# Projection Z and attention A of a hybrid diffusion block: two blocks of engine programs written as one

## The chip, the cores and the metric

The kernel runs on one core of one Trainium2 chip. The metric is the device time of one execution in microseconds (us). Three executions of the kernel before took 1727.18, 1730.48 and 1730.88 us, median 1730.48. A fourth one was profiled: it took 1729.09 us, of which its trace spans 1727.3 us.

The engines are named as in the profile: PE is TensorE (matmuls and transposes), PEld its weight loads, DVE is VectorE, ACT is ScalarE, POOL is GpSimd, SP is the sync engine, which here issues DMAs. Each engine runs its own list of instructions in order and waits on semaphores for the others. A wait at the head of an engine's list holds up everything that stands behind it in that list.

## The reference

One layer of a transformer: 128 context tokens and 512 latent tokens (640 in all, five tiles of 128), D_MODEL 1024. What matters here:

```python
z = h @ lw['w_in']
q_a, k_a, v_a, c_q, c_kv, k_r, g_a, g_b = jnp.split(z, cuts, axis=-1)
qa = rmsnorm(q_a.reshape(b, s, H_A, HD_A), lw['gqa_qn']).transpose(0, 2, 1, 3)
ka = rmsnorm(k_a.reshape(b, s, KV_A, HD_A), lw['gqa_kn']).transpose(0, 2, 1, 3)
...
qa = apply_rope(qa, *rope_a)              # latent tokens only
...
o_a = block_attention(...)                # attention A: 8 heads, 2 key heads, 128 wide
...
qb = (cq @ lw['w_qb'])...                 # queries of attention B
o_b = block_attention(...)                # attention B
merged = sigmoid(g_a) * (o_a @ w_oa) + sigmoid(g_b) * (o_b @ w_ob)
x = x + g1 * (merged @ w_out)
x = x + g2 * moe_ffn(...)                 # 64 small experts and a shared one
```

Context tokens attend to context keys only (128 columns of scores), latent tokens to 128 cached keys and 512 latent ones (640 columns).

## The kernel before

The kernel is a row of blocks. In each block every engine has one program, and all engines meet at the block's end. The blocks around the change are Z (lines 422 to 720), attention A and attention B (one function, `attend`, line 749; A is called first), and a block between A and B that expands B's keys.

**Z** computes the first 1984 columns of `w_in` in four chunks (`CHUNKS`: queries of heads 0 to 3, keys and values, the latent columns, queries of heads 4 to 7) and for five token tiles each: 20 units, `UNITS[i] = (chunk, tile)`, in this order. Unit i goes through these steps:
- `project(i)` on PE (line 451): 24 matmuls of 512 columns into PSUM bank i % 4.
- `squares(i)` on ACT (line 515), `sums(i)` on DVE (line 626), a power on POOL (line 594): the reciprocal norms.
- `apply(i)` on DVE (line 641): norm, gain and rotation, five vector operations for queries. It ends with semaphore `s_zn`.
- `turn(i)` on PE (line 472): four transposes into bank 4 + i % 2, semaphore `s_zT`.
- `untangle(i)` on ACT (line 538): one copy out of PSUM into `qT`, semaphore `s_ze`.

They are staggered: on PE `turn(i - 2)` follows `project(i)`, on DVE `apply(i - 1)` follows `sums(i)`, on ACT `untangle(i - 3)` follows `squares(i)`. So after `project(19)` each engine still has a tail: `turn(17)`, `turn(18)`, `turn(19)` on PE, `apply(18)` and `apply(19)` on DVE, `untangle(16)` to `untangle(19)` on ACT. Units 18 and 19 are tiles 3 and 4 of the last chunk: queries of heads 4 to 7. The split of heads 0 and 1 into high and low parts is made in Z by POOL (lines 602 to 604).

**A** works on 40 tiles n = (head, token tile), `N = 40`, with `lag = 2`. For each n:
- PE, loop at line 896: `scores(n)`, `turn_p(n - 2)` (transposes of the probabilities), `values(n - 3)` (probabilities times values), and at the last tile of a head, for heads 0 to 4, `rope_rows(h)` (line 819): four f32 matmuls of 512 columns with the weights `wqb`, for attention B.
- ACT, loop at line 949: `take_p(n - 2)`, `softmax(n)` (the exponential with a row sum), and the copies of a finished output.
- DVE, loop at line 1127: `maximum(n)`, `take_p(n - 2)`, `normalise(n)` (a reciprocal and a scaling).
- `maximum(n)` waits for `scores(n)`, `softmax(n)` for `maximum(n)`, `normalise(n)` for `softmax(n)`.
- PSUM: scores lie in banks 0 and 1 or 2 and 3 in turn (the 128 columns of tile 0 in bank 0 or 2), transposed probabilities in banks 4 and 5, outputs in bank 6 (`pO`) and bank 7 (`pC`, `rope_rows`).

`wqb` (1.5 MB) is loaded by SP at the start of A's block, line 795. Its place in SBUF is that of Z's scratch rows (`zq`, `zn`, `zt`, `rot`), so it can't be loaded before Z's rows are done with. `rope_rows(0)` waits for the load (`s_wqb`, line 822).

Of the kernel before, what the change touches and what calls it, by code (L numbers as in the profile page):

```python
# [26 lines left out]
F32 = mybir.dt.float32  # L27
# [7 lines left out]
P = 128  # L35
# [59 lines left out]
def build(nc, I, O, S, ctx):  # L95
# [326 lines left out]
    with nc.Block() as block:  # L422
        @block.sync
        def _(sp):
            sp.dma_start(wz[1], w_in_v[:, :, C_KA:C_KA + 512]).then_inc(s_wz[1], 16)
            for g in range(KVA):
                sp.dma_start(cache[:, g * HD:(g + 1) * HD], I["cache_gqa_k"][0, 0, g]).then_inc(s_cache, 16)
                sp.dma_start(vA[:, 1, g, :], I["cache_gqa_v"][0, 0, g]).then_inc(s_vc, 16)
            sp.dma_start(cache[:, 256:384], I["cache_mla_ckv"][0, 0]).then_inc(s_cache, 16)
            for c in (384, 448):  # L430
                sp.dma_start(cache[:, c:c + ROPE], I["cache_mla_krope"][0, 0]).then_inc(s_cache, 16)
            sp.dma_start(kgB, I["mla_kva_g"].to_broadcast([P, KVL])).then_inc(s_cache, 16)
            sp.dma_start(wkvb, I["w_kvb"][0]).then_inc(s_wkvb, 16)

            sp.wait_ge(s_z, NT)
            sp.dma_start(wz[0][:, :, 0:448], w_in_v[:, :, C_CQ:C_CQ + 448]).then_inc(s_wz[2], 16)
            sp.wait_ge(s_z, 2 * NT)
            sp.dma_start(wz[1], w_in_v[:, :, 512:1024]).then_inc(s_wz[3], 16)

            sp.wait_ge(s_zn, NT + 1)  # L440
            for g in range(KVA):
                sp.dma_start(O["gk"][0, 0, g], zo[0][:, g * HD:(g + 1) * HD]).then_inc(s_out, 16)
                sp.dma_start(O["gv"][0, 0, g], vA[:, 0, g, :]).then_inc(s_out, 16)
            sp.wait_ge(s_zn, 2 * NT + 1)
            sp.dma_start(O["ckv"][0, 0], zo[1][:, 256:256 + KVL]).then_inc(s_out, 16)
            sp.dma_start(O["kr"][0, 0], zo[1][:, 384:384 + ROPE]).then_inc(s_out, 16)
            sp.wait_ge(s_out, 16 * 6)

        @block.tensor
        def _(pe):  # L450
            def project(i):

                c, t = UNITS[i]
                w, b = CHUNKS[c][2], c % 2
                if i >= 4:

                    pe.wait_ge(s_zn, i - 3)
                if c == 0:
                    pe.wait_ge(s_hl, t + 1)
                elif t == 0:  # L460
                    pe.wait_ge(s_wlP, 4 + KT * c)
                out = bank(i % 4)[:, 0:w]
                for k in range(KT):
                    if i == 0:
                        pe.wait_ge(s_wlP if k % 2 else s_wlV, k // 2 + 1)
                    xh, xl = hHi[:, k, t * P:(t + 1) * P], hLo[:, k, t * P:(t + 1) * P]
                    pe.matmul(out, xh, zHi[b][:, k, 0:w], start=(k == 0), stop=False)
                    pe.matmul(out, xl, zHi[b][:, k, 0:w], start=False, stop=False)
                    mm = pe.matmul(out, xh, zLo[b][:, k, 0:w], start=False, stop=(k == KT - 1))
                mm.then_inc(s_z, 1)  # L470

            def turn(i):

                pe.wait_ge(s_zn, i + 1)
                if i >= 2:
                    pe.wait_ge(s_ze, i - 1)
                    if remainder_of(i - 2):
                        pe.wait_ge(s_zl, remainder_of(i - 2))
                kind = CHUNKS[UNITS[i][0]][0]
                src = out_rows(i)  # L480
                for j in range({"q": 4, "kv": 2, "lat": 4}[kind]):
                    tr = pe.transpose(bank(4 + i % 2)[:, j * P:(j + 1) * P], src[:, j * P:(j + 1) * P], ident[:, :])
                tr.then_inc(s_zT, 1)

            def turn_cache():

                pe.wait_ge(s_cache, 16 * 6)
                for j in range(4):
                    tr = pe.transpose(bank(6)[:, j * P:(j + 1) * P], cache[:, j * P:(j + 1) * P], ident[:, :])
                tr.then_inc(s_zc, 1)  # L490

            n = len(UNITS)
            for i in range(n):
                project(i)
                if i == 1:
                    turn_cache()
                if i >= 2:
                    turn(i - 2)
            turn(n - 2)
            turn(n - 1)  # L500

        @block.scalar
        def _(act):
            def rows_hi(t):

                act.activation(hHi[:, :, t * P:(t + 1) * P], hT[:, :, t * P:(t + 1) * P], ACT.Copy).then_inc(s_hh, 1)

            def weights_hi(c, k0, k1):

                w, b = CHUNKS[c][2], c % 2  # L510
                act.wait_ge(s_wz[c], 16)
                for k in range(k0, k1):
                    act.activation(zHi[b][:, k, 0:w], wz[b][:, k, 0:w], ACT.Copy).then_inc(s_wh, 1)

            def squares(i):

                c, t = UNITS[i]
                kind = CHUNKS[c][0]
                n = {"q": 512, "kv": 256, "lat": 448}[kind]
                act.wait_ge(s_z, i + 1)  # L520
                if i >= 2:

                    act.wait_ge(s_zm, i - 1)
                if kind == "kv":
                    act.activation(vA[:, key_col(t) // P, :, :].rearrange("p g d -> p (g d)"),
                                   bank(i % 4)[:, 256:512], ACT.Copy)
                act.activation(zq[i % 2][:, 0:n], bank(i % 4)[:, 0:n], ACT.Square).then_inc(s_zq, 1)

            def take_latent(ps, col):

                act.activation(ckvT[:, col:col + P], ps[:, 2 * P:3 * P], ACT.Copy)
                return act.activation(krHH[:, col:col + P], ps[:, 3 * P:4 * P], ACT.Copy)

            def take_keys(ps, col):

                return act.activation(kHiA[:, :, col:col + P], ps[:, 0:256].rearrange("p (g t) -> p g t", g=KVA), ACT.Copy)

            def untangle(i):

                c, t = UNITS[i]  # L540
                kind = CHUNKS[c][0]
                act.wait_ge(s_zT, i + 1)
                ps = bank(4 + i % 2)
                if kind == "q":
                    h = 4 * (c // 3)
                    ins = act.activation(qT[:, h:h + 4, t * P:(t + 1) * P], ps.rearrange("p (h t) -> p h t", h=4),
                                         ACT.Copy)
                elif kind == "kv":
                    ins = take_keys(ps, key_col(t))
                else:  # L550
                    for j in range(2):
                        act.activation(cqT[:, j, t * P:(t + 1) * P], ps[:, j * P:(j + 1) * P], ACT.Copy,
                                       scale=cols[:, 80 + j:81 + j])
                    ins = take_latent(ps, key_col(t))
                ins.then_inc(s_ze, 1)

            rows_hi(0)
            weights_hi(0, 0, KT)
            rows_hi(1)
            n = len(UNITS)  # L560
            for i in range(n):
                c, t = UNITS[i]
                if i + 2 < NT:
                    rows_hi(i + 2)
                squares(i)
                if i == 1:
                    act.wait_ge(s_zc, 1)
                    take_keys(bank(6), P)
                    take_latent(bank(6), P).then_inc(s_cc0, 1)
                if i >= 3:  # L570
                    untangle(i - 3)
                if t in AHEAD and c < 3:

                    if c == 0 and t == 3:
                        act.wait_ge(s_gd, 1)
                    weights_hi(c + 1, *AHEAD[t])
            for i in range(n - 3, n):
                untangle(i)

        @block.gpsimd  # L580
        def _(pool):
            def weights_lo(c, ks):

                w, b = CHUNKS[c][2], c % 2
                for k in ks:
                    pool.wait_ge(s_wh, KT * c + k + 1)
                    pool.tensor_tensor(zLo[b][:, k, 0:w], wz[b][:, k, 0:w], zHi[b][:, k, 0:w].bitcast(F32),
                                       ALU.subtract).then_inc(s_wlP, 1)

            weights_lo(0, range(1, KT, 2))  # L590
            for i, (c, t) in enumerate(UNITS):
# [3 lines left out]
                if t in AHEAD and c < 3:  # L595
                    weights_lo(c + 1, range(*AHEAD[t]))
# [1807 lines left out]
```

## Time and profile before

| | us |
|---|---|
| executions | 1727.18, 1730.48, 1730.88 (median 1730.48) |
| the profiled execution | 1729.09 |
| its span | 1727.3 |
| PE busy | 1551.4 (90%) |
| DVE busy | 1016.0 (59%) |
| ACT busy | 724.5 (42%) |
| POOL busy | 652.3 (38%) |
| last matmul of Z's projection starts | 178.19 |
| first matmul of A | 187.70 |

The profile names each instruction by its line in the kernel. Times start at the span's start. Busy time is the time in which an engine executed; the idle time in front of an instruction is given in square brackets with the instruction that ended it. PEclk is the share of TensorE's full clock that was granted: 1.0 is 2.4 GHz, 0.5 is 1.2 GHz.

### The profile page before, as it was taken

The page shows a single profiled execution, that of the slowest core. Times are in us where ns is not written, and L with a number is a line of the kernel's source. Part 1 is how long each engine was busy: PE and PEld are TensorE (multiplying, and loading weights), DVE is VectorE, ACT ScalarE, POOL GpSimd, SP SyncE. Part 2 cuts the span into 40 slices and gives each one's busy share as a digit, 9 for nine tenths or more (in the row PEclk, how much of TensorE's full clock was granted, in tenths as well). Part 3 has the DMA queues.
Part 4 walks back from the last instruction along what each step waited for, and adds up shares of the span by engine and source line. Part 5 has one row for each costly group of instructions (what it writes and reads, how often), then busy time and mean ns, then how long its engine had stood idle before and what let it go on. Part 6 is the DMA issues. An engine that isn't in the chain of part 4 may idle for free. (4 is left out here: it accounts for less than half of the span.)

```text
span 1727.3 us, 22786 instructions
## 1 busy us (share of the span) xinstructions
PE 1551.4 (90%) x7699; PEld 1169.3 (68%) x7699; DVE 1016.0 (59%) x1595; ACT 724.5 (42%) x1067; POOL 652.3 (38%) x727
## 2 busy tenths in 40 slices
PE   7799788799989999999896999999999999999992
PEld 2678687688879989964443766666666666666671
DVE  1966687666675565526643665555555555555554
ACT  2422343333442122202213565555555555555560
POOL 0445275322213233300452454344443434444561
PEclk9899899999999999999998999999999999999996
DMA  9320100000035464544174999999999999999954
GB/s 323 100 91 10 37 1 1 1 1 2 1 99 147 140 213 135 146 163 147 59 283 180 335 363 365 353 343 338 352 347 351 343 338 340 339 330 335 344 188 185
DMA packets 130282, 352.66 MB, mean 204 GB/s; under 512 B 22165, under 2 KB 77849, under 8 KB 103193
## 3 DMA queue, kind: packets, MB, share of 16 engines
q1 hardware_dynamic: 98488, 237.87, 37.8%
q10 hardware_dynamic: 10288, 71.86, 11.2%
q0 software_dynamic: 21440, 42.08, 9.7%
q8 instruction: 38, 0.62, 0.2%
q14 instruction: 28, 0.22, 0.0%
HBM read 335.53 MB, written 48.32 MB: 222 GB/s over the span
## 5 line engine op out<-in xcount | busy, mean ns | idle before, releaser
L2289 DVE TENSOR_TENSOR e_wlo<-mem,e_whi 128x2048 fp32r<-128x2048 f32 x140 | 314.6, 2289 | 98.6 <-ACT e_whi L2224 98.6
L2224 ACT ACTIVATE e_whi<-mem 128x2048 fp32r<-128x2048 f32 x140 | 260.2, 1913 | 24.4 <-DMA mem<-in_w_e 16.9
L2194 PE MATMUL psum<-mem 128*128 128x512 f32 x560 | 252.1, 593 | 2.1 <-ACT mem L2256 2.1
L2174 PE MATMUL psum<-e_whi,e_xhi 128*128 128x512 f32 x560 | 228.2, 408 | 7.1 <-DVE e_xlo L2296 7.1
L2176 PE MATMUL psum<-e_wlo,e_xhi 128*128 128x512 f32 x560 | 222.2, 397 | 0.0
L2175 PE MATMUL psum<-e_whi,e_xlo 128*128 128x512 f32 x560 | 222.0, 396 | 0.0
L2132 POOL TENSOR_TENSOR held<-nhalf 1x1 f32<-1x1 f32 x206 | 116.7, 567 | 261.3 <-DMA sums<-mem,si 104.4
L2194 PEld LDWEIGHTS psum<-mem 128*128 128x128 f32 x560 | 101.1, 190 | 103.0 <-issue 102.9
L1494 POOL TENSOR_TENSOR w_lo<-mem,w_hi 128x1024 fp32r<-128x1024 f32 x30 | 76.1, 2560 | 163.6 <-ACT w_hi L1438 163.6
L2296 DVE TENSOR_TENSOR e_xlo<-psum,e_xhi 128x512 fp32r<-128x512 f32 x140 | 90.2, 686 | 76.7 <-ACT e_xhi L2230 76.7
L2306 DVE TENSOR_TENSOR mem<-mem,psum 128x256 f32<-128x256 f32 x70 | 42.5, 607 | 151.0 <-ACT mem L2263 151.0
L2174 PEld LDWEIGHTS psum<-e_whi,e_xhi 128*128 128x128 f32 x560 | 105.8, 189 | 30.0 <-DVE e_xlo L2296 7.8
L2176 PEld LDWEIGHTS psum<-e_wlo,e_xhi 128*128 128x128 f32 x560 | 105.6, 189 | 25.5
L2175 PEld LDWEIGHTS psum<-e_whi,e_xlo 128*128 128x128 f32 x560 | 106.0, 189 | 22.3
L939 ACT ACTIVATE mem<-psum,small 128x640 f32<-128x640 f32 (+1 forms) x80 | 60.3, 754 | 130.4 <-DVE small L1106 87.9
L2182 PE MATMUL psum<-ident,mem 128*128 128x128 f32 x560 | 76.3, 280 | 43.1 <-DMA mem<-h,gi 34.4
L2230 ACT ACTIVATE e_xhi<-psum 128x512 fp32r<-128x512 f32 x140 | 76.0, 595 | 78.4 <-PE psum L2182 78.4
L2182 PEld LDWEIGHTS psum<-ident,mem 128*128 128x128 f32 x560 | 62.1, 142 | 68.0 <-DMA mem<-h,gi 56.0
L1513 DVE SCALAR_TENSOR_TENSOR mem<-mem,cols 128x256 f32<-128x256 f32 x256 | 107.7, 497 | 0.0
L1438 ACT ACTIVATE w_hi<-mem 128x1024 fp32r<-128x1024 f32 x30 | 30.2, 1054 | 165.2 <-DMA mem<-in_w_ob 90.8
L2147 POOL DMA_INDIRECT mem<-h,gi x68 | 75.9, 1116 | 36.4 <-issue 36.4
L1420 PE MATMUL psum<-h_hi,w_hi 128*128 128x320 f32 x256 | 81.7, 319 | 2.0 <-PEq L1149 2.0
(320 smaller groups left out, 3272.8 us busy)
## 6 DMA issues: line engine op xcount, KB each, us to landing
mem<-in_w_e SPq DMA_DIRECT2D x144, 1024.0 KB, 12.3
mem<-in_w_e ACTq DMA_DIRECT2D x66, 1024.0 KB, 11.2
mem<-in_w_mod SPq DMA_DIRECT2D x24, 1024.0 KB, 12.0
mem<-in_w_in SPq DMA_DIRECT2D x16, 512.0 KB, 4.5
mem<-in_w_in SPq DMA_DIRECT2D x3, 2048.0 KB, 8.8
sums<-mem SPq DMA_DIRECT2D x10, 512.0 KB, 4.7
mem<-sums SPq DMA_DIRECT2D x10, 512.0 KB, 5.4
mem<-in_x_sample SPq DMA_DIRECT2D x8, 512.0 KB, 11.0
```

The lines of the kernel that those rows point to most:

```text
L1420: pe.matmul(out, whi[b][:, q, k, :], hi[:, k, cols_], start=(k == 0), stop=False)
L1494: pool.tensor_tensor(wlo[b][:, q, :, :], wraw[b][:, q], whi[b][:, q, :, :].bitcast(F32), ALU.subtract).then_inc(sg["wl"], 1)
L1513: ins = dve.scalar_tensor_tensor(out=macc[b][y], in0=wmh[b][:, k, :], scalar=cols[:, k + 8 * y:k + 8 * y + 1], in1=brow[b] if k == 0 else ...
L2132: pool.tensor_tensor(held[:, c:c + 1], nhalf[0:1, 0:1], nhalf[0:1, 0:1], ALU.add)
L2174: pe.matmul(out, xh, wh, start=first, stop=False)
L2175: pe.matmul(out, xl, wh, start=False, stop=False)
L2176: return pe.matmul(out, xh, wl, start=False, stop=last)
L2182: tr = pe.transpose(pX[:, k * P:(k + 1) * P], xg[u % 2][:, k * P:(k + 1) * P], ident[:, :])
L2194: mm = pe.matmul(pY[:, cs], gT[:, f, :], w2[v][:, f, cs], start=(f == 0), stop=(f == 1))
L2224: act.activation(wHi13[u % 2][:, a], w13[u][:, a], ACT.Copy).then_inc(se["h13"], 1)
L2289: dve.tensor_tensor(wLo13[u][:, a], w13[u][:, a], wHi13[u % 2][:, a].bitcast(F32), ALU.subtract)\
L2296: dve.tensor_tensor(xLo[:, 4 * h:4 * h + 4, :].rearrange("p k t -> p (k t)"), pX[:, 512 * h:512 * (h + 1)], xHi[:, 4 * h:4 * h + 4, :].bit ...
```

## The change

Z's programs are no longer a block. They become functions (`zed_sync`, `zed_tensor`, `zed_scalar`, `zed_gpsimd`, `zed_vector`) that A's block calls at the head of each engine's program. Their text is the same, indented one level less, save for what follows.
- Units 18 and 19 are projected into banks 7 and 6 and transposed back into the same banks (`zbank`, `tbank`).
- The tail is cut. PE's Z program ends after `turn(17)`, DVE's after `sums(19)`, ACT's after `untangle(17)`.
- In A's loops `apply(18)` and `apply(19)` stand at the end of DVE's steps n = 1 and n = 2. `turn(18)` and `turn(19)` stand on PE in steps 3 and 4, between `turn_p(n - 2)` and `values(n - 3)`. `untangle(18)` and `untangle(19)` stand on ACT in steps 3 and 4 behind `softmax(n)`.
- New waits: `scores` of heads 0 and 1 wait for POOL's split (`s_qs`); `values(0)`, which writes bank 7, waits for `untangle(18)` and `values(1)`, which writes bank 6, for `untangle(19)`; POOL's split of head 4 waits for `untangle(19)`; SP's load of `wqb` waits for `turn(19)` (`s_zT` at 20).

The diff without the changes of indentation:

```diff
-    with nc.Block() as block:
-        @block.sync
-        def _(sp):
+    def zbank(i):
+        return bank(i % 4 if i < 18 else 25 - i)
+
+    def tbank(i):
+        return bank(4 + i % 2) if i < 18 else zbank(i)
+
+    def zed_sync(sp):
...
-                out = bank(i % 4)[:, 0:w]
+            out = zbank(i)[:, 0:w]
...
-            turn(n - 2)
-            turn(n - 1)
+        return turn
...
-            for i in range(n - 3, n):
-                untangle(i)
+        untangle(n - 3)
+        return untangle
...
-                    pool.wait_ge(s_qs, h + 1)
-                    pool.tensor_tensor(qLoA[:, h, :], qT[:, h, :], qHiA[h][:, :].bitcast(F32), ALU.subtract)
+                pool.wait_ge(s_qs, 2 * h + 1)
+                pool.tensor_tensor(qLoA[:, h, :], qT[:, h, :], qHiA[h][:, :].bitcast(F32), ALU.subtract)\
+                    .then_inc(s_qs, 1)
...
-                if i >= 1:
+            if 1 <= i < n - 1:
                     apply(i - 1)
...
-            apply(n - 1)
+        return apply
...
+        LASTZ = len(UNITS)
...
                 def _(sp):
+                    zed_sync(sp)
+                    sp.wait_ge(s_zT, LASTZ)
                     sp.dma_start(wqb, I["w_qb"][0].rearrange("(k p) n -> p k n", p=P)).then_inc(s_wqb, 16)
...
             def _(pe):
+                turn_z = None if mla else zed_tensor(pe)
...
                     elif t == 0 and h >= 2:
                         pe.wait_ge(s["ql"], h - 1)
+                    elif t == 0:
+                        pe.wait_ge(s_qs, 2 * h + 2)
...
+                        if not mla and h == 0:
+                            pe.wait_ge(s_ze, LASTZ - 1)
                         pe.matmul(pC, v[:, 0, :], pTc, start=True, stop=True).then_inc(s["C"], 1)
                         return
                     pe.wait_ge(s["TeA"], late(n))
+                    if t == 1 and not mla and h == 0:
+                        pe.wait_ge(s_ze, LASTZ)
...
                     if lag <= n < N + lag:
                         turn_p(n - lag)
+                    if not mla and n in (3, 4):
+                        turn_z(LASTZ + n - 5)
                     if n > lag:
                         values(n - lag - 1)
...
+                    if not mla and n in (3, 4):
+                        untangle_z(LASTZ + n - 5)
                     if n > lag:
                         h, t = TILES[n - lag - 1]
...
                         qh, ql, _ = q_of(h)
+                        if h == 4:
+                            pool.wait_ge(s_ze, LASTZ)
...
+                        if not mla and n in (1, 2):
+                            apply_z(LASTZ + n - 3)
                         if not mla and t == 2 and 1 <= h <= NT:
                             row_sums(h - 1)
```

## Rows read from the trace of the kernel before

**Rows 1.** Stretches of Z and of A: length, busy us (count) by engine, PEclk, DMA share, GB/s

```profile
170.00:178.00 8.00, 8.00 (x39) 6.54 (x38) 5.81 (x10) 1.09 (x2) 2.58 (x2) 1.00 0.00 0
187.60:335.00 147.40, 128.63 (x894) 116.48 (x894) 109.88 (x200) 62.26 (x152) 75.88 (x62) 0.99 0.03 12
```

**Rows 2.** Timeline of the seam: start us, us, engine, line, operation [idle before <-releaser]

```profile
178.43 0.60 PE L482 MATMUL psum<-ident,mem 128*128 128x128 f32 x4
179.12 1.08 ACT L546 ACTIVATE mem<-psum 128x512 f32<-128x512 f32 x2
...
179.98 0.17 DVE L639 TENSOR_SCALAR small<-small 128x4 f32<-128x4 f32 x1
...
182.79 0.68 DVE L666 TENSOR_TENSOR mem<-psum,small 128x512 f32<-128x512 f32 x1
...
184.90 0.69 DVE L672 TENSOR_TENSOR mem<-mem 128x512 f32<-128x512 f32 x1
...
185.65 1.12 PE L482 MATMUL psum<-ident,mem 128*128 128x128 f32 x4 [1.61 <-DVE mem L672]
186.80 0.60 ACT L546 ACTIVATE mem<-psum 128x512 f32<-128x512 f32 x1 [2.13 <-PE psum L482]
187.65 0.39 SPq L795 DMA_DIRECT2D mem<-in_w_qb  x1
187.66 1.28 ACT L939 ACT_TABLE_LOAD   x1 [0.27 <-PEq L422]
...
188.61 0.29 DVE L1102 TENSOR_REDUCE small<-psum 128x1 f32<-128x128 f32 x1 [3.02 <-PE psum L854]
...
190.32 0.82 DVE L1102 TENSOR_REDUCE small<-psum 128x1 f32<-128x640 f32 x1 [0.38 <-PE psum L854]
```

**Rows 3.** A's steps 1 to 3 on ACT and DVE, same view

```profile
191.18 0.79 ACT L939 ACTIVATE mem<-psum,small 128x640 f32<-128x640 f32 x1 [1.76 <-DVE small L1102]
...
192.10 0.16 DVE L1113 RECIPROCAL small<-small 128x1 f32<-128x1 f32 x1 [0.95 <-ACT mem L939]
...
192.29 0.55 DVE L1115 TENSOR_SCALAR mem<-mem,small 128x640 f32<-128x640 f32 x1
...
195.20 0.82 DVE L1102 TENSOR_REDUCE small<-psum 128x1 f32<-128x640 f32 x1
```

**Rows 4.** Scores of 640 columns, first and last of six matmuls: steps 1 and 3

```profile
188.38 0.57 PE L852 MATMUL psum<-ka_hi,qa_hi 128*128 128x320 f32 x1
...
189.81 0.47 PE L854 MATMUL psum<-ka_lo,qa_hi 128*128 128x320 f32 x1
...
194.64 0.39 PE L852 MATMUL psum<-ka_hi,qa_hi 128*128 128x320 f32 x1
...
195.46 0.31 PE L854 MATMUL psum<-ka_lo,qa_hi 128*128 128x320 f32 x1
```

**Rows 5.** TensorE's clock around the seam, columns as in rows 1

```profile
180.50:182.50 2.00, 0.00 (x0) 0.00 (x0) 1.93 (x5) 0.00 (x0) 0.73 (x1) 0.64 0.00 0
...
190.00:191.30 1.30, 1.30 (x7) 1.30 (x6) 0.82 (x1) 0.12 (x1) 0.00 (x0) 0.50 0.91 383
191.30:192.00 0.70, 0.49 (x4) 0.22 (x2) 0.00 (x0) 0.70 (x2) 0.00 (x0) 0.99 1.02 430
```

**Rows 6.** A's step 4 and the start of step 5, columns as in rows 2

```profile
196.72 0.74 PE L869 MATMUL psum<-ident,mem 128*128 128x128 f32 x5 [0.95 <-issue]
...
197.63 0.82 DVE L1102 TENSOR_REDUCE small<-psum 128x1 f32<-128x640 f32 x1
...
198.41 1.88 PE L825 MATMUL psum<-mem 128*128 128x512 f32 x4
...
200.61 0.29 DVE L1102 TENSOR_REDUCE small<-psum 128x1 f32<-128x128 f32 x1 [0.45 <-PE psum L854]
```

**Rows 7.** The load of wqb, issued at 187.65

```profile
DMA to landing us min/median/max: 6.4/6.4/6.4
```

**Rows 8.** SP's next issue behind it, in attention B

```profile
477.18 0.39 SPq L791 DMA_DIRECT2D mem<-in_w_in  x1
```

More of the change, by code:

```diff
@@ new lines, in zed_tensor, with project, turn, turn_cache @@
+    def zed_tensor(pe):
+        def project(i):
+            c, t = UNITS[i]
+            w, b = CHUNKS[c][2], c % 2
+            if i >= 4:
+                pe.wait_ge(s_zn, i - 3)
+            if c == 0:
+                pe.wait_ge(s_hl, t + 1)
+            elif t == 0:
+                pe.wait_ge(s_wlP, 4 + KT * c)
+            out = zbank(i)[:, 0:w]
+            for k in range(KT):
+                if i == 0:
+                    pe.wait_ge(s_wlP if k % 2 else s_wlV, k // 2 + 1)
+                xh, xl = hHi[:, k, t * P:(t + 1) * P], hLo[:, k, t * P:(t + 1) * P]
+                pe.matmul(out, xh, zHi[b][:, k, 0:w], start=(k == 0), stop=False)
+                pe.matmul(out, xl, zHi[b][:, k, 0:w], start=False, stop=False)
+                mm = pe.matmul(out, xh, zLo[b][:, k, 0:w], start=False, stop=(k == KT - 1))
+            mm.then_inc(s_z, 1)
+        def turn(i):
+            pe.wait_ge(s_zn, i + 1)
+            if i >= 2:
+                pe.wait_ge(s_ze, i - 1)
+                if remainder_of(i - 2):
+                    pe.wait_ge(s_zl, remainder_of(i - 2))
+            kind = CHUNKS[UNITS[i][0]][0]
+            src = out_rows(i)
+            for j in range({"q": 4, "kv": 2, "lat": 4}[kind]):
+                tr = pe.transpose(tbank(i)[:, j * P:(j + 1) * P], src[:, j * P:(j + 1) * P], ident[:, :])
+            tr.then_inc(s_zT, 1)
+        def turn_cache():
+            pe.wait_ge(s_cache, 16 * 6)
+            for j in range(4):
+                tr = pe.transpose(bank(6)[:, j * P:(j + 1) * P], cache[:, j * P:(j + 1) * P], ident[:, :])
+            tr.then_inc(s_zc, 1)
+        n = len(UNITS)
+        for i in range(n):
+            project(i)
+            if i == 1:
+                turn_cache()
+            if i >= 2:
+                turn(i - 2)
+        return turn
@@ new lines, in zed_scalar, with rows_hi, weights_hi, squares @@
+    def zed_scalar(act):
+        def rows_hi(t):
+            act.activation(hHi[:, :, t * P:(t + 1) * P], hT[:, :, t * P:(t + 1) * P], ACT.Copy).then_inc(s_hh, 1)
+        def weights_hi(c, k0, k1):
+            w, b = CHUNKS[c][2], c % 2
+            act.wait_ge(s_wz[c], 16)
+            for k in range(k0, k1):
+                act.activation(zHi[b][:, k, 0:w], wz[b][:, k, 0:w], ACT.Copy).then_inc(s_wh, 1)
+        def squares(i):
+            c, t = UNITS[i]
+            kind = CHUNKS[c][0]
+            n = {"q": 512, "kv": 256, "lat": 448}[kind]
+            act.wait_ge(s_z, i + 1)
+            if i >= 2:
+                act.wait_ge(s_zm, i - 1)
+            if kind == "kv":
+                act.activation(vA[:, key_col(t) // P, :, :].rearrange("p g d -> p (g d)"),
+                               zbank(i)[:, 256:512], ACT.Copy)
+            act.activation(zq[i % 2][:, 0:n], zbank(i)[:, 0:n], ACT.Square).then_inc(s_zq, 1)
+        def take_latent(ps, col):
+            act.activation(ckvT[:, col:col + P], ps[:, 2 * P:3 * P], ACT.Copy)
+            return act.activation(krHH[:, col:col + P], ps[:, 3 * P:4 * P], ACT.Copy)
+        def take_keys(ps, col):
+            return act.activation(kHiA[:, :, col:col + P], ps[:, 0:256].rearrange("p (g t) -> p g t", g=KVA), ACT.Copy)
+        def untangle(i):
+            c, t = UNITS[i]
+            kind = CHUNKS[c][0]
+            act.wait_ge(s_zT, i + 1)
+            ps = tbank(i)
+            if kind == "q":
+                h = 4 * (c // 3)
+                ins = act.activation(qT[:, h:h + 4, t * P:(t + 1) * P], ps.rearrange("p (h t) -> p h t", h=4),
+                                     ACT.Copy)
+            elif kind == "kv":
+                ins = take_keys(ps, key_col(t))
+            else:
+                for j in range(2):
+                    act.activation(cqT[:, j, t * P:(t + 1) * P], ps[:, j * P:(j + 1) * P], ACT.Copy,
+                                   scale=cols[:, 80 + j:81 + j])
+                ins = take_latent(ps, key_col(t))
+            ins.then_inc(s_ze, 1)
+        rows_hi(0)
+        weights_hi(0, 0, KT)
+        rows_hi(1)
+        n = len(UNITS)
+        for i in range(n):
+            c, t = UNITS[i]
+            if i + 2 < NT:
+                rows_hi(i + 2)
+            squares(i)
+            if i == 1:
+                act.wait_ge(s_zc, 1)
+                take_keys(bank(6), P)
+                take_latent(bank(6), P).then_inc(s_cc0, 1)
+            if i >= 3:
+                untangle(i - 3)
+            if t in AHEAD and c < 3:
+                if c == 0 and t == 3:
+                    act.wait_ge(s_gd, 1)
+                weights_hi(c + 1, *AHEAD[t])
+        untangle(n - 3)
+        return untangle
@@ L1061, in _ @@
             def _(dve):
+                apply_z = None if mla else zed_vector(dve)
                 def mean(h):
```

374 lines of the change are left out of this document (136 added, 238 removed).

## Prediction

> **What bounds the kernel now.** I read the stretches first, then the timeline of the seam between Z and A, then the clock, last the load of wqb. Z's projection keeps PE busy without a gap at the full clock: 8.00 of 8.00 us [rows 1]. A does not hang on PE's arithmetic but on a loop between DVE and ACT: maximum, exponential, reciprocal, scaling, next maximum. From maximum(2), which follows the scaling of 192.29 to 192.84, to maximum(3) at 195.20 it takes some 2.4 us a tile [rows 3]. So an instruction added to DVE's list in A costs its whole length, and PE costs something only where it comes late.
>
> Between the two lies the seam. `project(19)` and `turn(17)` end at 179.03. DVE goes on with `apply(18)` and `apply(19)` until 185.59, `turn(19)` ends at 186.77, ACT's `untangle(19)` at 187.40, A's block starts at 187.65, and DVE has its first maximum at 188.61 after 3.02 us of idleness. Then it waits 0.38 us more for PE, whose clock has fallen [rows 2, 5]. The 8.46 us from 180.15 (end of `sums(19)`) to 188.61 are thus 5.44 us of `apply` and 3.02 us of wait. The change can win the 3.02 and 0.38 at most; the `apply` work is moved, not removed.
>
> What is late by x us at the start of A makes the whole kernel late by x. SP's next issue stands at 477.18, behind A, in attention B [rows 8], and each block meets all engines at its end. I see nothing that would take it up.
>
> **The change, step by step.** I follow the new order with durations from the rows and put the result beside the times of before.
>
> DVE and ACT, steps 0 to 3. DVE is free at 180.15. `scores(0)` stands on PE right behind `turn(17)` (179.03) and needs under 1 us, so maximum(0) runs at 180.15 to 180.44. ACT is free at 180.20 and loads the exponential's table, 1.28 us [rows 2], until 181.50; before, this load lay beside PE's first scores. exp(0) (0.37 + 0.19 in the trace, some 0.5 overlapped, my estimate) ends at 182.0, reciprocal and scaling at 182.5. maximum(1) 0.82, exp(1) 0.92 with its row sum (191.18 to 192.10), reciprocal and scaling 0.74 [rows 3] end at 185.0. `apply(18)` takes 2.80 (182.79 to 185.59 for its twin [rows 2]), to 187.8. maximum(2), exp(2), normalise(2) take 2.55, to 190.4; `take_p(0)` lies in the wait for exp(2). `apply(19)` 2.80, to 193.2. maximum(3) runs at 193.2 to 194.0, where it was at 195.20 [rows 3]. Up to here the change **gains 2.0 us**.
>
> PE, step 3. PE waits in `turn_p(1)` for DVE's `take_p(0)` at 189.0, turns, does `turn(18)`, and stands in `values(0)`, which now waits for `untangle(18)`. This stands on ACT behind exp(3), which needs maximum(3): exp(3) ends at 194.95, the copy takes 0.60, PE goes on at 195.6. Queued behind `values(0)` are `scores(4)`. DVE would want them at 195.75 (exp(3), reciprocal, scaling). What they take depends on the clock. In the trace it fell in the idle stretch 180.5 to 182.5 (0.64 on the mean, PE idle since 179.03), and work from 187.70 on brought it back at 191.3 [rows 2, 5]. Here PE is idle from some 185.4 to 189.0 and from 191 to 195.6. I take 1.2 GHz. Six scores matmuls then take 1.90 (188.38 to 190.28), at 2.4 GHz 1.13 (194.64 to 195.77) [rows 4]; `values(0)` some 0.4. S(4) comes at 198.0 (197.1 at the full clock). maximum(4) starts at 198.0 against 197.63 before [rows 6]: the gain is gone, **+0.4**.
>
> PE, step 4. `turn_p(2)`: five transposes, 0.74 at the full clock [rows 6], some 1.35 at the half (four took 1.12 against 0.60 [rows 2]), to 199.35. `turn(19)` 0.6 to 1.1, its semaphore at 200.1. Only now may SP issue wqb: before, it did so at 187.65, and the 6.4 us to landing [rows 7] were over at 194.05, 4.4 us before `rope_rows(0)` at 198.41 [rows 6]. This cover is gone. Now it lands at 200.1 + 0.1 + 6.4 = 206.6. In the meantime `untangle(19)` behind exp(4) ends at 201.15 and `values(1)` at some 202.3. Then PE stands at `rope_rows(0)` for 4.3 us with all of head 1's scores queued behind it, and DVE and ACT wait for them.
>
> `rope_rows(0)` starts at 206.65 instead of 198.41: +8.2. After 4.3 us of idleness I take the half clock for its four matmuls of 512 columns. At the full clock they and the small `scores(5)` took 2.20 us (198.41 to maximum(5) at 200.61 [rows 6]), of which I give some 1.7 to the four; at the half clock these take twice as long: +1.7. maximum(5) comes at 210.6 instead of 200.61: **+10.0**. From there on every engine's order and distance is as before, with the clock back.
>
> Costed at nothing, with their cover: `scores(0)` and `scores(1)` wait for POOL's split, which POOL makes during units 16 and 17 of Z; POOL's split of head 4 waits for `untangle(19)`, at some 201, and isn't due for two heads; SP's other waits ahead of wqb are for units 5 and 10 of Z and their stores, long done; units 18 and 19 in other banks cost the same; one meeting of all engines less is in the 3.02. Bounds for what the trace doesn't show: the clock at `scores(4)` and at `rope_rows(0)` (the sum is +6.5 with 2.4 GHz at both, +8.2 at `rope_rows` alone with it, +10.0 with neither), and the load, alone on the queue as before, within 1 us of 6.4 to either side. A table load behind a busy ACT could also cost some wait in ACT's pipeline; at least 0, at most the 1.28 of the load again, since nothing longer of its kind is in the rows.
>
> The Trainium skill speaks against this order, in "DMA: Bandwidth & Descriptors", section "Rules for kernel authors": issue the DMA early, compute, and wait on its semaphore late, so that the fixed cost overlaps. The trace of before does this with 4.4 us to spare; the change issues the load immediately ahead of the one instruction that needs it.
>
> Of the exponential's table, the page "ScalarE: Activation LUTs", section "What ACT_TABLE_LOAD costs" of the Trainium skill, says about 2.66 us per switch, a drain of 1.38 included. The row has 1.28 and the exponential directly behind it; with the page's figure exp(0) and all that follows would come 1.4 later, and the sum would be +11.4. I keep the row's.
>
> The sum against the profiled execution: 1729.09 + 10.0 = 1739.1. This execution lies 1.4 below the median of the three; the mean of all four is 1729.4, which gives 1739.4. I say 1739.5.
>
> **The rivals.**
> (a) The load is exposed, but PE keeps the full clock at one or both places. For it: PE has short pieces of work in steps 1 to 3. Against it: the clock fell in the trace within 4 us of idleness [rows 5]. +6.5 to +8.2: 1736 to 1737.6.
> (b) The load is not what PE waits for, because it lands sooner or is issued sooner than I read. Then `rope_rows(0)` follows `values(1)` at 202.3 instead of 198.41: +3.9, 1733.3. Against it: 6.4 us measured, and the text of the wait.
> (c) Not slower: the turns moved into A are fully covered. The mechanism would be that DVE, not PE, is the last to be ready in steps 3 to 5, and only the gain of 2.0 stays: 1727.4. For it: DVE is A's bound over the stretch as a whole. It decides at `rope_rows(0)`: only if wqb lands before `values(1)` ends and `scores(4)` and `scores(5)` are done before DVE asks (195.75 and 198.3) is there no loss. Against it: both waits of PE are for copies that stand behind DVE's own chain, so PE can't be early.
> (d) A later stage takes up the delay (a stage bound by weight loads that begin at a fixed time): about 0, 1729.4. Against it: SP issues nothing between 187.65 and 477.18 [rows 8].
>
> **How the numbers follow.** The load exposed, half clock: 0.65. (a) 0.18. (b) 0.06. (c) 0.07. (d) 0.04. About 0.2%, 3.5 us, is what can be told from no change. The forecast and (a) are slower, 0.83, of (b) 0.04 is: 0.87. (c) at -2.0 is mostly within the bound, as are (d) and the rest of (b): same 0.09; faster 0.04, for (c) with the whole 3.4 us won. The range: executions of one kernel spread by 3.7 us, terms of the load and of the table by 1 to 1.4 each. From 1734, which takes in (a) and half of (b), to 1743.5: about 0.85.
>
> **What would show it.** In the profile after: wqb is issued right behind the last of the L482 transposes, about 12 us later than before and some 13 us after DVE's first maximum; PE has one idle piece of over 3 us that a DMA ends, in front of the first L825 matmul; PEclk is 0.5 around it; DVE's first maximum at about 180.2, its fourth at 193.2 or so, its sixth at about 210.6. Between A's sixth maximum and the end of A nothing changes its length. I'd be wrong if the first L825 matmul stood within 5 us of its old time, if PE's idle piece in front of it ended with an ACT copy, or if A's end moved by less than its sixth maximum.

## The result and the profile after

The changed kernel took 1738.75 us (median of 4 executions, 1735.91 to 1740.83) against 1729.87 for the kernel before (4 executions, 1727.18 to 1730.88). The ratio is 1.0053 with a 95% interval of 1.0034 to 1.0072: slower by half a per cent, some 9 us. The forecast was 1739.5, with 10.0 us for the seam. The profiled execution of the changed kernel took 1735.91, the shortest of its four, with a span of 1734.1.

The timeline of the seam in the changed kernel (start us, us, engine, line, operation [idle before <-releaser]; line 1126 is the maximum that stood at 1102, 666 the first product of `apply`, 547 `untangle`, 485 `turn`, 894 `values(0)`, 903 `values(1)`, 831 `rope_rows`), to be read against [rows 2, 3, 6]:

```profile
178.13 0.17 DVE L639 TENSOR_SCALAR small<-small 128x4 f32<-128x4 f32 x1
178.21 0.28 DVE L1126 TENSOR_REDUCE small<-psum 128x1 f32<-128x128 f32 x1
178.38 1.28 ACT L955 ACT_TABLE_LOAD   x1
...
180.16 0.16 DVE L1137 RECIPROCAL small<-small 128x1 f32<-128x1 f32 x1 [1.67 <-ACT mem L955]
...
183.00 0.68 DVE L666 TENSOR_TENSOR mem<-psum,small 128x512 f32<-128x512 f32 x1
...
188.16 0.68 DVE L666 TENSOR_TENSOR mem<-psum,small 128x512 f32<-128x512 f32 x1
...
190.88 0.82 DVE L1126 TENSOR_REDUCE small<-psum 128x1 f32<-128x640 f32 x1
...
192.52 0.59 ACT L547 ACTIVATE mem<-psum 128x512 f32<-128x512 f32 x1
...
193.25 0.77 PE L894 MATMUL psum<-mem 128*128 128x128 f32 x2 [4.21 <-ACT mem L547]
...
195.66 0.82 DVE L1126 TENSOR_REDUCE small<-psum 128x1 f32<-128x640 f32 x1 [2.25 <-PE psum L862]
196.48 1.06 PE L485 MATMUL psum<-ident,mem 128*128 128x128 f32 x4
...
197.62 0.39 SPq L799 DMA_DIRECT2D mem<-in_w_qb  x1
198.41 2.47 PE L903 MATMUL psum<-mem 128*128 128x128 f32 x10 [0.87 <-ACT mem L547]
205.15 3.78 PE L831 MATMUL psum<-mem 128*128 128x512 f32 x4 [4.27 <-DMA mem<-in_w_qb]
...
209.36 0.29 DVE L1126 TENSOR_REDUCE small<-psum 128x1 f32<-128x128 f32 x1 [10.80 <-PE psum L862]
```

The reader is to see four things. DVE no longer idles 3.02 us between Z and A: its first maximum follows the last sums at once. PE stands 4.21 us for `untangle(18)` and then makes the fifth maximum 2.25 us late. SP issues wqb only when `turn(19)` has ended, and PE waits 4.27 us for its landing. DVE, which had waited 0.45 us there, waits 10.80.

Two lines say how long the load took from issue to landing and where SP's next issue stands, against 6.4 [rows 7] and 477.18 [rows 8]:

```profile
DMA to landing us min/median/max: 7.5/7.5/7.5
```

```profile
484.78 0.39 SPq L793 DMA_DIRECT2D mem<-in_w_in  x1
```

TensorE's clock in the changed kernel (length, busy us and count by engine, PEclk, DMA share, GB/s), against [rows 5]:

```profile
178.00:180.20 2.20, 0.41 (x4) 0.15 (x2) 0.49 (x4) 2.10 (x4) 1.01 (x1) 1.00 0.00 0
180.20:182.40 2.20, 1.29 (x8) 1.01 (x8) 1.21 (x4) 0.88 (x2) 0.00 (x0) 0.85 0.00 0
182.40:185.00 2.60, 1.92 (x6) 1.51 (x6) 2.53 (x6) 0.00 (x0) 0.00 (x0) 0.50 0.00 0
...
200.90:205.10 4.20, 0.00 (x0) 0.00 (x0) 0.00 (x0) 0.00 (x0) 0.00 (x0) 0.50 0.57 235
205.10:209.00 3.90, 3.85 (x6) 1.79 (x7) 0.00 (x0) 0.00 (x0) 0.00 (x0) 0.50 0.00 0
```

It fell from 2.4 to 1.2 GHz at about 181.7 (which gives the mean of 0.85 in the second row). PE had been idle for 1.79 us, had worked from 180.18 to 181.43, and stood in a second gap, of 0.91 us. From 182.4 to 209.0 the mean PEclk is 0.50, so `values(1)`, the wait for the load and `rope_rows(0)` all lie at 1.2 GHz.

**One measure for all kernels.** The change touches little in front of the last sums of Z (two units use other banks) and nothing behind A's sixth maximum. So I measure the seam, from the start of the last L639 of Z to the start of A's sixth maximum. Before it is 200.61 - 179.98 = 20.63 us; after, 209.36 - 178.13 = 31.23: **+10.60**. From the sixth maximum to A's fortieth and last there are 95.66 us before and 95.67 after, so the later tiles take nothing up. The two spans differ by less (+6.8). Z's last sums came 1.85 us earlier in the profiled execution of the changed kernel (178.13 against 179.98), so the sixth maximum is 8.75 later. These 1.85 us arise where the clock differed in Z's first units: mean PEclk was 0.73 from 50 to 60 us and 0.85 from 90 to 100, against 0.59 and 0.71 before. No run ties them to the merge: the last sums stand at 179.98 and 179.43 in the two kernels with the old border, and between 177.96 and 180.04 in the eight merged ones. SP's issue in attention B is 7.60 later, so another 1.15 went behind A's sixth maximum. The stage behind A ran at a mean PEclk of 0.93 in the one execution (296 to 345 us) and 0.99 in the other (305 to 353), which fits, but no run tests it.

### The profile page after: what moved, and what is told of

Read it like the earlier page. It is cut to its first block and busy times, and to the rows that moved or that the text cites. A ratio compares the mean times of both kernels' runs of the same rounds, so it can differ in the third digit from the quotient of the medians.

```text
span 1734.1 us, 22778 instructions
## 1 busy us (share of the span) xinstructions
PE 1550.7 (89%) x7699; PEld 1169.1 (67%) x7699; DVE 1016.7 (59%) x1595; ACT 730.6 (42%) x1067; POOL 666.8 (38%) x727
## 5 line engine op out<-in xcount | busy, mean ns | idle before, releaser
L2158 POOL TENSOR_TENSOR held<-nhalf 1x1 f32<-1x1 f32 x206 | 126.7, 615 | 259.9 <-DMA sums<-mem_h,si 106.0
L903 PE MATMUL psum<-mem 128*128 128x128 f32 x640 | 83.9, 280 | 0.9 <-ACT mem L547 0.9
```

Source lines behind the costliest of these rows:

```text
L903: mm = pe.matmul(pO[:, (t - 1) * P:t * P], v[:, kt, :], pT[:, j, (t - 1) * P:t * P], start=(j == 0), stop=(j == 4))
L2158: pool.tensor_tensor(held[:, c:c + 1], nhalf[0:1, 0:1], nhalf[0:1, 0:1], ALU.add)
```

## The experiments

All seams below are from profiles of single executions. The work from the sixth maximum to the last, which no experiment touches, takes 95.6 to 95.8 us in every one of them. The seam itself varies more, because the clock does. The changed kernel and experiments 1, 3, 4 and 5 give PE the same work up to A's third scores, but the clock fell 3.6, 4.6, 3.7, 3.8 and 4.8 us behind Z's last sums. In experiment 1 it was back before `values(1)`, in the changed kernel and experiment 3 not, after the same work of PE. Where that matters, the text below says how much. Whole times tell less: executions of the kernel before spread from 1724.3 to 1732.2 beside the first four experiments and from 1724.0 to 1738.3 beside the others. L639 and the maximum carry other line numbers in each kernel; the sixth maximum of each is shown at the end.

**1. The rotary part of wqb early.** On the changed kernel:

```diff
+    wqr = mem.at(M_R + 9728, 2, HB, ROPE)
...
+        sp.wait_ge(s_z, 3 * NT)
+        for k in range(2):
+            sp.dma_start(wqr[:, k], I["w_qb"][0, k * P:(k + 1) * P].rearrange("p (h c) -> p h c", h=HB)[:, :, NOPE:NOPE + ROPE])\
+              .then_inc(s_wqr, 16)
...
-                        pe.wait_ge(s_wqb, 16)
+                        pe.wait_ge(s_wqr, 32)
...
-                                       wqb_rope[:, k], start=(k == 0), stop=(k == 1))
+                                       wqr[:, k], start=(k == 0), stop=(k == 1))
...
+                    pool.wait_ge(s_wqb, 16)
```

> The changed kernel with one thing taken off its path: the 64-column parts of the rotary queries in wqb (0.5 MB), which are all that rope_rows reads, are loaded into a place of their own as soon as unit 14 is projected; the whole wqb is loaded as in the changed kernel and waited for by POOL's late split alone. Measure: the seam, from the start of the last L639 of Z (sums(19)) to the start of A's sixth maximum: 20.63 us in the kernel before, 31.23 in the changed one. My theory (the load of wqb behind turn(19) is what PE waits for, 4.3 us of idleness plus a fallen clock): rope_rows(0) follows values(1) at once, the seam is 24.9, the time about 6 us below the changed kernel and some 3 to 4 above the kernel before. Rival (the waits for untangle(18) and untangle(19) are the cost, the load only lies beside them): the seam stays over 29 and the time within 2 us of the changed kernel.

Measured: seam 23.57 us, 7.66 below the changed kernel and 2.94 above the kernel before. Time: 1.0034 of the kernel before (1.0021 to 1.0048), some 5.9 us, where I had expected 3 to 4. PE in this kernel:

```profile
193.29 0.77 PE L899 MATMUL psum<-mem 128*128 128x128 f32 x2 [4.21 <-ACT mem L552]
...
196.46 0.60 PE L490 MATMUL psum<-ident,mem 128*128 128x128 f32 x4
198.34 1.35 PE L908 MATMUL psum<-mem 128*128 128x128 f32 x10 [1.28 <-ACT mem L552]
199.53 1.88 PE L836 MATMUL psum<-mem 128*128 128x512 f32 x4
```

`rope_rows(0)` (L836) now follows `values(1)` (L908) without a wait, at 1.88 us instead of 3.78. The two waits for copies (4.21 and 1.28) are still there. The rival that made the load a bystander falls.

The 7.66 us are three parts: 4.27 of PE's wait for the load, 2.00 from the start of `rope_rows(0)` to the sixth maximum at the faster clock, and 1.39 up to the end of `values(1)`. The third isn't the load's: the clock was back before `values(1)` (0.60 for `turn(19)`, 1.35 for `values(1)`, against 1.06 and 2.47), by nothing that the edit changes on PE. That is also why I had the seam 1.3 too long. And since the clock was up already, this run does not tell whether the 2.00 us are owed to the wait. Of the 10.60 us it gives the load 4.27 for certain and up to 6.27.

**2. The late load alone.** On the kernel before:

```diff
                 def _(sp):
+                    sp.wait_ge(s["T"], 3)
                     sp.dma_start(wqb, ...
```

> The kernel before with the load of wqb alone made late: SP waits for turn_p(2) of A (the third group of transposed probabilities) before it issues the load. Nothing else of the change. Theory (the late load alone costs what the change costs, less the waits for the copies): issue at about 197.5, landing 6.4 to 7.5 later, rope_rows(0) at about 204.5 instead of 198.41, its four matmuls at half clock: the seam (last L639 of Z to A's sixth maximum) 28.4 to 29.5 instead of 20.63, the time 8 to 9 us above the kernel before. Rival (the load is hidden or its delay is taken up by A's later tiles): seam up, but the distance of A's last maximum to Z's last L639 (116.3 us) within 2 us of before.

Measured: seam 28.35, +7.72; last maximum 124.14 us behind Z's last sums instead of 116.29, +7.85. Time: 1.0030 (1.0018 to 1.0041), some 5.2 us, where I had expected 8 to 9. PE and the clock:

```profile
203.43 3.78 PE L826 MATMUL psum<-mem 128*128 128x512 f32 x4 [5.42 <-DMA mem<-in_w_qb]
```

```profile
191.20:200.80 9.60, 4.95 (x35) 4.19 (x34) 6.46 (x14) 3.69 (x11) 0.00 (x0) 1.00 0.30 92
201.30:203.40 2.10, 0.00 (x0) 0.00 (x0) 0.00 (x0) 0.00 (x0) 0.00 (x0) 0.50 0.57 237
```

Nothing but the moment of one DMA's issue was changed, and the five maxima ahead of it stand where they stood before. So here all of the 7.72 us is the late load: `rope_rows(0)` starts 5.57 later (PE's wait is 5.42), and 2.15 come from the clock, which was at 2.4 GHz until some 3 us into the wait and let the four matmuls take 3.78 instead of 1.88 [rows 6]. Nothing of it is taken up later in A. That experiment 1 took away nearly the same, 7.66, is partly chance: the issue stands 1.99 us earlier behind Z's last sums here than in the changed kernel, the load was 1 us shorter, and 1.39 of the 7.66 were not the load's.

**3. PE kept at work in front of the load.** On the changed kernel:

```diff
+                    pe.wait_ge(s["Ce"], t + 1)
                     if t == 0:
+                        for _ in range(28):
+                            pe.transpose(bank(7)[:, 0:P], ident[:, :], ident[:, :])
                         pe.wait_ge(s_wqb, 16)
-                    pe.wait_ge(s["Ce"], t + 1)
```

> The changed kernel with 28 more transposes of the identity on PE, into bank 7, between values(1) and the wait for wqb, so that PE works while it would wait for the load (rope_rows(0) overwrites that bank). Theory (the clock has fallen by then and costs 1.7 to 2 us): PEclk stays at 1.0 in front of rope_rows(0), its four matmuls take 1.9 us instead of 3.8, the seam falls from 31.23 to 29.3. Rival (what is slow there is not the clock): the seam stays at 31.2 or above it by what the transposes run over the load's landing.

Measured: seam 29.26, 1.97 shorter. Time: 1.0050 (1.0034 to 1.0066). PE and the clock:

```profile
204.97 1.98 PE L833 MATMUL psum<-mem 128*128 128x512 f32 x4 [0.39 <-DMA mem<-in_w_qb]
```

```profile
200.90:204.90 4.00, 3.68 (x28) 3.44 (x26) 0.00 (x0) 0.00 (x0) 0.00 (x0) 0.84 0.54 219
204.90:207.00 2.10, 2.02 (x7) 1.07 (x7) 0.00 (x0) 0.00 (x0) 0.00 (x0) 1.00 0.00 0
```

28 transposes that compute nothing shorten the kernel's seam by 2 us: the four matmuls behind the load ran at 2.4 GHz. They did not keep the clock, as I had expected, but brought it back: it had been at 1.2 GHz since 181.7 and rose at about 202.2, while they ran. So 1.97 of the 10.60 us are the clock at `rope_rows(0)`. In the changed kernel it had fallen long before the wait; experiment 2 is the one that shows a fall inside it.

**4. The turns one place earlier.** On the changed kernel, on PE and in the same way on ACT (`untangle_z` ahead of `take_p` and `softmax`):

```diff
+                    if not mla and n in (3, 4):
+                        turn_z(LASTZ + n - 5)
                     if lag <= n < N + lag:
                         turn_p(n - lag)
-                    if not mla and n in (3, 4):
-                        turn_z(LASTZ + n - 5)
```

> The changed kernel with the moved turns one place earlier: in A's steps 3 and 4 PE does turn(18), turn(19) ahead of turn_p(n - 2), and ACT does untangle(18), untangle(19) ahead of take_p(n - 2) and softmax(n). The load of wqb still follows turn(19). Theory: turn(19) ends right behind apply(19), about 4 us sooner against Z's end, the load is issued and lands as much sooner, scores(4) no longer waits for untangle(18): the seam is 25 to 26.5 instead of 31.23, and rope_rows(0) still starts when the load lands. Rival (the chain of DVE and ACT, not PE's place in it, sets step 4): S(4) and the fifth maximum come no earlier, the seam within 1 us of 31.23.

Measured: seam 24.20, 7.03 shorter; the fifth maximum 15.19 us behind Z's last sums instead of 17.53. Time: 1.0025 (1.0015 to 1.0035). wqb is issued at 192.05, and:

```profile
198.30 3.28 PE L831 MATMUL psum<-mem 128*128 128x512 f32 x4 [2.67 <-DMA mem<-in_w_qb]
```

The wait for the load is still there and 1.60 shorter. That `turn_z` came a place earlier removed the 2.25 us at the fifth maximum and pulled the load's issue forward by 5.40 against Z's end. I had expected 25 to 26.5. The load took 6.25 us from issue to PE's start here, where it had taken 7.53; these 1.28 us and 0.35 behind the load's landing are no part of what the earlier place does, as far as the rows show. So 5.40 of the 7.03 are the edit's.

**5. Both.** Experiments 1 and 4 together.

> The early load of the rotary part of wqb (first experiment) and the turns one place earlier (fourth) together, on the changed kernel. Theory (two costs, one behind the other on PE: 7.7 us of exposed load, and some 2.9 of waits for copies, the latter mostly at scores(4)): rope_rows(0) starts where it would have in the fourth experiment without its wait of 2.67 us, seam 19.9 us with PE at full clock and 21.6 at half, against 20.63 in the kernel before, 31.23 in the changed one. Rival (the merge costs something else too, so that the seam can't come under that of before): seam 22 or more.

Measured: seam 20.20, 0.43 below the kernel before. Time: 0.9999 (0.9984 to 1.0013). Alone the two edits gave 7.66 and 7.03, together 11.03 and not 14.69: the earlier turn had won most of its time by an earlier load, which is off the path here. Some 1.5 us of the missing 3.66 are the clock's: from the start of `values(1)` to the sixth maximum it took 4.91 us, in experiment 1 3.40. PEclk was 0.76 and 0.77 in step 4 and in `rope_rows(0)`:

```profile
190.80:195.60 4.80, 3.44 (x18) 3.03 (x19) 4.02 (x9) 2.60 (x7) 0.00 (x0) 0.76 0.51 163
195.60:198.00 2.40, 2.40 (x8) 1.17 (x7) 0.38 (x1) 0.00 (x0) 0.00 (x0) 0.77 0.82 337
```

**6. The exponential's table early.** On experiment 5, ACT's program of Z:

```diff
+            if i == 7:
+                act.activation(small[:, 127:128], nhalf[:, 0:1], ACT.Exp)
             squares(i)
```

> The previous kernel with the exponential's table loaded early: ACT does one exponential of one column in Z, ahead of squares(7), so that the table load (1.28 us, at 178.38 to 179.66 in the changed kernel, with DVE waiting 1.67 us for the first exponential) isn't at the seam. Theory: exp(0) starts right behind maximum(0), the second maximum is 1.1 us earlier against Z's last L639 (1.3 instead of 2.43) and the seam 0.5 to 1.1 shorter than in the previous kernel. Rival (the squares and copies of Z need another table, so that a second load comes): the second maximum stays at 2.4 or is later, with two more loads in the trace.

Measured: second maximum 1.29 us behind Z's last sums instead of 2.43, seam 18.01. Time: 0.9992 (0.9974 to 1.0009). The trace has one table load in Z and none at the seam:

```profile
106.15 1.28 ACT L572 ACT_TABLE_LOAD   x1
```

So the merge had put this load, which lay beside PE's first scores before, on the path, at 1.14 us. Squares and copies went on with the exponential's table. The seam fell by 2.19 us, more than the 1.14 and more than the 0.5 to 1.1 that I had expected. The rest is the clock's: mean PEclk from 177 to 196 was 0.82 in this execution and 0.75 in the one of experiment 5, and from the start of `values(1)` to the sixth maximum PE took 3.78 us instead of 4.91. Whether the edit or chance gave this execution the better clock, no run tells.

**7. PE kept at work through the seam.** On experiment 6, 36 transposes of the identity in PE's gaps of steps 1 to 4:

```diff
+                        if not mla and n in (1, 3, 4):
+                            if n == 4:
+                                pe.wait_ge(s["TeA"], 1)
+                            spin({1: 5, 3: 14, 4: 12}[n], 1 if n == 1 else 5)
...
+                        if not mla and n == lag:
+                            spin(5, 5)
```

> The previous kernel with 36 transposes of the identity on PE in its gaps of A's steps 1 to 4 (5, 5, 14 and 12), into PSUM columns that nothing reads, so that PE's clock doesn't fall while DVE does apply(18) and apply(19). Theory (the fallen clock is what still makes PE late at the fifth and sixth maximum): PEclk 1.0 from Z's end through step 5, turn_p(2), values(1) and rope_rows(0) at 0.74, 1.28 and 1.9 us, the seam 17.0 to 17.8, some 3 us below the kernel before, and the time 2 to 4 us below it. Rival (PE's order, not its clock, is late): the seam within 0.5 of the previous kernel.

Measured: seam 17.54. Time: 0.9987 (0.9973 to 1.0002). The clock stayed up:

```profile
179.00:198.00 19.00, 15.64 (x108) 12.77 (x108) 14.47 (x32) 6.61 (x19) 1.01 (x1) 1.00 0.22 83
```

The seam lies within the theory's 17.0 to 17.8, but only 0.47 below experiment 6, which the rival had allowed too. The run doesn't tell them apart: experiment 6 had come out below its own forecast already and left little. PE was still 0.97 us late for DVE at full clock, so its order has a part in what is left.

**8. `apply` in pieces.** On experiment 7: pieces of `apply(18)` and `apply(19)` ahead of `normalise(0)`, `(1)` and `(2)`, where DVE waits for an exponential. The gaps of PE shrink with it, so its idle transposes are 19 (5, 5, 6 and 3) instead of 36:

```diff
+                        if not mla and n < 3:
+                            apply_z(*((LASTZ - 2, (0,)), (LASTZ - 2, (1,)), (LASTZ - 1, (0,)))[n])
                         normalise(n)
...
-                            apply_z(LASTZ + n - 3)
+                            apply_z(*((LASTZ - 2, (2,)), (LASTZ - 1, (1, 2)))[n - 1])
```

> The previous kernel (rotary part of wqb early, turns first, table early, PE kept busy) with apply(18) and apply(19) cut in pieces that stand where DVE waits for an exponential: the first product of apply(18) behind maximum(0), its two half rotations behind maximum(1), the first product of apply(19) behind maximum(2), each ahead of normalise; the rest behind normalise(1) and normalise(2). PE's idle transposes are 5, 5, 6 and 3. Theory (apply's whole length lies on the loop of maximum, exponential and scaling, which leaves DVE 0.5, 0.95 and 0.75 us of wait in steps 0 to 2): the seam falls from 17.54 to between 15.8 and 16.4 us, 4 to 5 below the kernel before, the time 3 to 5 us below it (0.2 to 0.3%). Rival (PE's order is what is late at the sixth maximum, DVE's earlier readiness is lost in a wait): the seam stays within 0.4 of 17.5, with more idle time ahead of the sixth maximum.

Measured: seam 15.61 us, 5.02 below the kernel before and 15.62 below the changed one; I had expected 15.8 to 16.4. Time: 0.9975 of the kernel before (0.9953 to 0.9998), the only one of the eight whose interval lies below 1, and by a hair. DVE in steps 1 and 2; ahead of step 1's reciprocal it had 0.95 us of wait in [rows 3]:

```profile
182.18 0.75 DVE L679 TENSOR_TENSOR mem<-mem 128x256 f32<-128x256 f32 x2
183.21 0.16 DVE L1162 RECIPROCAL small<-small 128x1 f32<-128x1 f32 x1 [0.28 <-ACT mem L979]
...
186.14 0.68 DVE L675 TENSOR_TENSOR mem<-psum,small 128x512 f32<-128x512 f32 x1
187.05 0.16 DVE L1162 RECIPROCAL small<-small 128x1 f32<-128x1 f32 x1 [0.23 <-ACT mem L979]
```

**The sixth maximum in each kernel**, the end of each seam, in the order of the experiments 1 to 8. The idle time ahead of it says how late PE's scores were for DVE:

```profile
201.74 0.29 DVE L1132 TENSOR_REDUCE small<-psum 128x1 f32<-128x128 f32 x1 [3.24 <-PE psum L867]
```

```profile
207.78 0.29 DVE L1103 TENSOR_REDUCE small<-psum 128x1 f32<-128x128 f32 x1 [8.18 <-PE psum L855]
```

```profile
207.28 0.29 DVE L1128 TENSOR_REDUCE small<-psum 128x1 f32<-128x128 f32 x1 [8.84 <-PE psum L864]
```

```profile
202.16 0.29 DVE L1126 TENSOR_REDUCE small<-psum 128x1 f32<-128x128 f32 x1 [6.49 <-PE psum L862]
```

```profile
198.47 0.29 DVE L1132 TENSOR_REDUCE small<-psum 128x1 f32<-128x128 f32 x1 [2.50 <-PE psum L867]
```

```profile
196.49 0.29 DVE L1134 TENSOR_REDUCE small<-psum 128x1 f32<-128x128 f32 x1 [1.44 <-PE psum L869]
```

```profile
197.18 0.29 DVE L1146 TENSOR_REDUCE small<-psum 128x1 f32<-128x128 f32 x1 [0.97 <-PE psum L869]
```

```profile
195.65 0.29 DVE L1151 TENSOR_REDUCE small<-psum 128x1 f32<-128x128 f32 x1 [0.97 <-PE psum L874]
```

From it go the last sums of Z at 178.17, 179.43, 178.02, 177.96, 178.27, 178.48, 179.64 and 180.04.

**Seams and times together.** As shares of the kernel before, the seams say 1.0017, 1.0045, 1.0050, 1.0021, 0.9998, 0.9985, 0.9982 and 0.9971. In six of the eight the interval of the measured ratio holds this share. Experiment 1 measured more (1.0034, from 1.0021) and experiment 2 less (1.0030, to 1.0041). From the sixth maximum to SP's issue in attention B the profiled executions of the ten kernels have 275.4 to 278.2 us, without an order by edit; I take the two misses for such differences of later stages, and that stays open.

## Why the prediction was right, step by step

Counted from the last sums of Z, so that Z's 1.85 us drop out:

| step | forecast | measured |
|---|---|---|
| fourth maximum, maximum(3) | 13.2 | 12.75 |
| fifth maximum | 18.0 | 17.53 |
| wqb issued | 20.2 | 19.49 |
| `rope_rows(0)` starts | 26.7 | 27.02 |
| sixth maximum | 30.6 | 31.23 |
| seam against before | +10.0 | +10.60 |

- The gain up to maximum(3): forecast 2.0, measured 15.22 - 12.75 = 2.47. The table load on the path was foreseen, and experiment 6 shows it there at 1.14 us: exp(0) began at 179.67, 1.29 us after the load's start at 178.38. The 2.66 us a switch of the Trainium skill ("ScalarE: Activation LUTs", section "What ACT_TABLE_LOAD costs") did not come here; the trace decides for 1.28.
- The loss of this gain at the fifth maximum: forecast 2.25 us of wait for `scores(4)` behind `untangle(18)`, measured 2.25. Experiment 4 takes it away: the fifth maximum stands at 15.19 there.
- The load: the place and the releaser were right. Experiment 2 shows its cost alone, 7.72, and experiment 1 that without it `rope_rows(0)` follows `values(1)` at once. One term was off: 7.5 us from issue to landing instead of 6.4. That `turn(19)` came 0.7 earlier than forecast nearly cancels it, by luck. That the idle time came out (forecast 4.3, measured 4.27) is luck too: the sum gave `values(1)` 1.15 us, as at the full clock, though it took the half clock for the work around it. `values(1)` took 2.47, and `untangle(19)` ended 1.03 earlier than forecast (20.14 us behind the last sums, not 21.17).
- The clock: half clock at `rope_rows(0)`, forecast as +1.7, shown by experiment 3 as 1.97. The size was right, the reason was not: I had given the 4.3 us of idleness as what makes `rope_rows(0)` slow, but the clock had fallen at 181.7 and never came back before the load had landed. The slow `values(1)` was hidden in the wait for the load. The slow `turn_p(2)` and `turn(19)` were not, since the load was issued behind them, and the sum had the first at the half clock, the second between the two. The Trainium skill says of waits for DMAs ("TensorE: Matmul & The Clock Gate", section "HAM oscillation — how this bites in real kernels") that PE is throttled in them and its next work starts slow. Experiment 2's rows agree: PEclk was 1.00 until some 3 us into a wait of 5.42 and 0.50 behind that. In the changed kernel PE was slow before the wait.
- Nothing later takes it up: the distance from the sixth maximum to the last is the same within 0.01 us. That ends rival (d). Rival (a), the full clock, ends with the rows of PEclk for the profiled execution. Experiment 1, where the clock was back before `values(1)`, shows that this clock is not the same in every execution; the other three of the changed kernel have no profile.
- Rival (b), +3.9 without the load's wait, is what experiment 1 built: +2.94. The missing 1 us is `values(1)` and its wait, which the better clock of that execution made shorter.
- Rival (c), not slower, does not hold for the change as it is, but it holds for the idea: with the load, the turns, the table and `apply` put where something covers them, the same merge wins 5.02 us at the seam. The prediction's ceiling of 3.02 and 0.38 us holds as long as `apply` stays whole (experiment 7: 3.09); cut in pieces it is in part covered, which the prediction had not thought of.
- One of its signs was misreckoned: wqb issued "some 13 us after DVE's first maximum". Its own times, 200.2 and 180.15, make 20; measured were 19.41.

That the whole time moved by 8.9 (medians) and not 10.6 is within the spread of executions, and that 1738.75 lies so near to 1739.5 is more than the terms deserve; the interval of 1.0034 to 1.0072 is 5.9 to 12.5 us.

## What to carry to other kernels

When two stages are merged, look at what the old border did besides costing its idle time: here it started a load as soon as the scratch rows under it were free, 10.8 us ahead of its use, and it let a table load lie beside PE's first work. A work item moved into a loop frees its buffers later by as much as it is moved, and every DMA into these buffers moves with it; the first reader of that DMA has to be looked for before anything is moved. And in an in-order queue the place of a moved item decides: the same two groups of transposes one place earlier brought the load's issue forward by 5.40 us.

## What the runs showed of the hardware

- The load of wqb (1.5 MB) took 6.4 us from issue to landing before and 7.5 after, and between 6.2 (experiments 4 and 8) and 7.9 (experiment 1) over the ten kernels. PE started behind it 6.25 us after its issue in experiment 4, 6.50 in experiment 2, 7.46 in experiment 3 and 7.53 in the changed kernel. What sets the difference of over a microsecond no run shows.
- TensorE's clock fell to 1.2 GHz at 181.7, 0.3 us into a gap of 0.91 us, which followed a gap of 1.79 us and 1.25 us of work. I had not expected this of gaps so short. With the same gaps experiment 5 kept 2.4 GHz until about 183.0, when PE was at work again. In experiment 7, with the gaps filled, it stayed at 2.4 GHz throughout.
- So the clock's moment differs between executions of the same work on PE, here by up to 1.2 us for the fall, and for the return by more: 18.2 us behind Z's last sums in experiment 1, 24.2 in experiment 3, 30.9 in the changed kernel. The first of these came before the work of the three differed. A difference of 1 to 1.5 us between single profiles can be this alone.
- The squares and copies of Z ran with the exponential's table loaded: after the one load at 106.15 no other came until 512, behind attention B.
